# A two-layer decoder trunk with gathered experts: seven gather buffers and nine kept weight chunks in place of eight and seven, with a weight computed per row and a reordered start and end

## What is computed

```
h = rmsnorm(x);  [p | q | k | v | gate logits] = h @ w_in          # 1024 -> 4096
A = pool_mixer(p)            # trailing means over 2/4/8/16 tokens minus the token, per-group map
B = attention(q, k, v) @ w_attn_up                                  # 8 heads, causal, ALiBi
x = x + (sigmoid(gA) * A + sigmoid(gB) * B) @ w_out
t = rmsnorm(x)
for each of 8 PEER heads:
    s = (t @ w_q)[2 halves] @ sub_keys.T           # 2 x 128 key scores
    sv, si = top_k(s, 16) of each half
    cv, ci = top_k(sv[0][:, None] + sv[1][None, :], 16)      # best 16 of 256 sums
    eid = si[0][..] * 128 + si[1][..];  g = softmax(cv)
x = x + sum over 8 heads * 16 experts of  g * gelu(u[eid] . t) * v[eid]
```

## Time and profile before

| | |
|---|---|
| the profiled execution's own time | 1624.07 us |
| its span, first to last instruction | 1622.3 us |
| median of three executions | 1621.58 us (1619.27 to 1624.75) |
| mean granted TensorE clock | 0.955 |
| moved by DMA | 653.94 MB, of which the gathers 536.90 MB |
| TensorE busy | 1323.5 us (82%) |
| VectorE busy | 1098.2 us (68%) |
| ScalarE busy | 756.4 us (47%) |
| GpSimd busy | 597.5 us (37%) |

### The profile page before, as it was taken

How to read it: one execution, slowest core, us unless ns; L and a number is a source line. 1 busy time by engine, 2 the same in 40 slices (tenths; PEclk the granted TensorE clock), 3 DMA queues, 4 the chain that set the end, 5 groups by cost and what they waited for, 6 DMA issues and landing times. The chain is left out here.

```text
span 1622.3 us, 18071 instructions
## 1 busy us (share of the span) xinstructions
PE 1323.5 (82%) x5612; PEld 814.4 (50%) x5612; DVE 1098.2 (68%) x2602; ACT 756.4 (47%) x2833; POOL 597.5 (37%) x516
## 2 busy tenths in 40 slices
PE   7997788888888696977888779888888877778776
PEld 7985456654554264653455436565555433233222
DVE  1057879766588687745567778867656777768545
ACT  1213535445544534424554454544464555555555
POOL 0012333345434332323533343233443444444552
PEclk9999999999999999989999999899999999999999
DMA  7859999999999999999999999999999999999996
GB/s 289 305 232 423 399 422 420 423 422 421 420 422 410 415 389 424 422 424 419 413 421 423 413 409 400 422 424 421 419 413 424 410 414 422 421 418 417 411 422 285
DMA packets 91800, 653.94 MB, mean 403 GB/s; under 512 B 10120, under 2 KB 11576, under 8 KB 12600
## 3 DMA queue, kind: packets, MB, share of 16 engines
q0 software_dynamic: 73728, 536.90, 80.2%
q1 hardware_dynamic: 17976, 115.89, 17.6%
HBM read 651.71 MB, written 1.05 MB: 402 GB/s over the span
## 5 line engine op out<-in xcount | busy, mean ns | idle before, releaser
L597 PE MATMUL ybank<-ring,diag 128*128 128x512 f32 x1668 | 828.2, 639 | 272.9 <-ACT diag L775 267.4
L1123 POOL DMA_INDIRECT ring<-in_uv,expert x512 | 597.3, 1167 | 1003.2 <-DVE xs L1014 435.3
L1001 DVE SCALAR_TENSOR_TENSOR ring<-ring,tok 128x1024 f32<-128x1024 f32 x512 | 620.8, 1225 | 390.7 <-DMA ring<-in_uv,expert 385.2
L597 PEld LDWEIGHTS ybank<-ring,diag 128*128 128x128 f32 x1668 | 314.4, 200 | 695.7 <-ACT diag L775 368.9
L747 ACT ACTIVATE sq<-dots 128x2 f32<-128x2 f32 (+1 forms) x257 | 52.2, 203 | 732.4 <-DVE ring L1001 732.3
L416 PEld LDWEIGHTS bank<-hT,wring 128*128 128x128 f32 x2432 | 291.6, 198 | 27.1 <-issue 27.1
L416 PE MATMUL bank<-hT,wring 128*128 128x128 f32 x2432 | 293.0, 281 | 4.9 <-DVE hT L904 4.9
L763 ACT ACTIVATE wgt<-th,half_p 128x1 f32<-128x1 f32 x512 | 170.3, 379 | 8.6
L775 ACT ACTIVATE diag<-cst,wgt 128x128 f32<-128x128 f32 x417 | 148.2, 392 | 5.2
L757 ACT ACTIVATE th<-arg,dots 128x1 f32<-128x1 f32 x512 | 122.9, 287 | 8.2
L1014 DVE SCALAR_TENSOR_TENSOR xs<-ring,wgt,xs 128x1024 f32<-128x1024 f32 x95 | 121.8, 1282 | 1.9 <-ACT wgt L763 1.8
(11 more groups left out here) (108 smaller groups left out, 681.7 us busy)
## 6 DMA issues: line engine op xcount, KB each, us to landing
wring<-in_chunks SPq DMA_DIRECT2D x92, 1024.0 KB
held<-in_chunks SPq DMA_DIRECT2D x14, 1024.0 KB, 18.6
ring<-in_uv,expert POOLq DMA_INDIRECT x512
xs<-in_x SPq DMA_DIRECT2D x2, 512.0 KB, 12.0
wpool<-in_w_pool SPq DMA_DIRECT2D x2, 512.0 KB, 13.9
trunk_out<-buf SPq DMA_DIRECT2D x4, 256.0 KB, 4.8
cst<-in_consts SPq DMA_DIRECT2D x1, 672.0 KB, 6.4
ring<-in_pool_scale SPq DMA_DIRECT2D x1, 512.0 KB, 8.5
```

Source lines behind the costliest of these rows:

```text
L597: ins = pe.matmul(ybank[m][:, :], diag[:, nth % DIAGS, :], ring[:, (2 * t + r) % RING, D + m * BANK:D + (m + 1) * BANK], start=(nth == ten ...
L1001: dve.scalar_tensor_tensor(out=ring[:, g % RING, 0:D], in0=ring[:, g % RING, 0:D], scalar=1.0, in1=tok[:, :], op0=ALU.mult, op1=ALU.mult, ...
L1123: pool.indirect_dma_start(ring[:, g % RING, :], None, uv, bass.IndirectOffsetOnAxis(ap=expert[:, w % 2, at:at + 1], axis=0)).then_inc(row_ ...
```

## The change

Numbers: `RING` 8 to 7, `HELD` 7 to 9. The kept chunks are then 16 to 24, which takes in the PEER query chunks of heads 0, 1 and 2. Small buffers make the room: `p_sb` shares `qT`, and keeps no first tile, since a new `carry` (128x64) holds what the first tile contributes to the first 16 tokens of the second; `kT` holds one tile, with the second tile's keys in `soft`; `rinv_all` lies in `buf2`; `prob` and `expert` have one window's place instead of two; the constant table loses 448 columns.

Weights of a row: `scalar_tick` runs the whole chain for row 0 when its own dot product is there, and then for row 1. Start: ScalarE issues `cst`, `beside` and `gains`. The query of head 0 runs in one piece behind the last transposes. The first eight experts come from the best 8 of each key half and 64 sums; the full search of head 0 follows, and its second eight experts are picked behind tick 0. End: in the last window TensorE first copies x into `ybank`, and `close_last` adds row 510 to `ybank` and then row 511.

```diff
-HELD = 7
+HELD = 9
-RING = 8
+RING = 7
...
-        first_heads = [(-10, -8, -6), (-2, 0, 1), (2, 3, 5), (7, 9, 10), (12, 13, 15), (17, 18, 20), (21, 23, 24),
+        first_heads = [(-10, -8, 0), (1, 2, 3), (4, 5, 6), (8, 9, 10), (12, 13, 15), (17, 18, 20), (21, 23, 24),
                        (26, 27, 29)]
-        first_queries = (-19, -17, -15, -13, -11, 0, 2, 4)
+        first_queries = (-19, -17, -15, -13, 0, 2, 4, 6)
...
+                        if r == 0 and k in (4, 6):
+                            pe.wait_ge(*read(w, f"g{k // 2 - 1}"))
...
-                side(0, a, range(6))
-                pe.wait_ge(x_mixed, OUTS * w + OUTS)
-                for j in range(2):
-                    ins = pe.transpose(g[:, j * P:(j + 1) * P], x_of(tile)[:, (6 + j) * P:(7 + j) * P], ident)
-                filled("g2", ins)
-                pe.wait_ge(*read(w, "g2"))
-                filled("pq0a", side(0, a, range(6, KC)))
+                filled("pq0a", side(0, claim("pq0a", a_done), range(KC)))
...
+            if tile == 0:
+                b = claim("carry", a_done)
+                for g in range(NG):
+                    lo = C_BEFORE + g * REACH
+                    ins = pe.matmul(b[:, g * REACH:(g + 1) * REACH], p_sb[:, g * P:(g + 1) * P], cst[:, lo:lo + REACH],
+                                    start=True, stop=True)
+                filled("carry", ins)
...
+                if tile == 0:
+                    pe.matmul(b[:, g * P:g * P + REACH], mine, cst[:, first:first + REACH], start=True, stop=True)
+                    ins = pe.matmul(b[:, g * P + REACH:(g + 1) * P], mine, cst[:, lo + REACH:lo + P],
+                                    start=True, stop=True)
...
+            if last and n == 0:
+                pe.wait_ge(x_mixed, OUTS * windows)
+                for m in range(2):
+                    pe.matmul(ybank[m][:, :], ident, x_of(w % NT)[:, m * BANK:(m + 1) * BANK], start=True, stop=False)
...
-            for rows in ((0,), (1,)) if t == windows * TICKS - 1 else ((0, 1),):
-                act.wait_ge(dot_done, 2 * t + rows[-1] + 1)
-                act_stepped(act.activation(sq[:, these], dots[:, c0:c0 + len(rows)], ACT.Square))
...
+            for r, c in enumerate(col):
+                act.wait_ge(dot_done, 2 * t + r + 1)
+                act_stepped(act.activation(sq[:, r:r + 1], dots[:, c:c + 1], ACT.Square))
...
+            def first_experts():
                 for r in range(2):
                     dve.wait_ge(*read(w, f"score0{'ab'[r]}"))
-                    key_search(0, (r,))
-                cand = best_sums(0)
+                    key_search(0, (r,), (0,))
+                sums = tmp[:, 0:64]
+                square = sums.rearrange("p (i j) -> p i j", i=8)
+                all_sums(square, 8)
+                search(lambda r: cv[:, :], lambda r: ci[:, :], lambda r: sums, range(1), (0,))
+                places(8, 3)
+                pick_of(0, 0, 8, square)
...
             if w == 0:
-                first_head()
+                yield head_tick(w, 0, 0)
+                first_experts()
+                key_search(0, eights=(8,))
+                yield head_tick(w, 0, 1)
+                sum_search(0)
+                weigh_heads(0)
+                yield head_tick(w, 0, 2)
+                pick_of(0, 8, 8, tmp[:, 0:P].rearrange("p (k i) -> p k i", i=TOPK))
...
+            t = windows * TICKS - 1
             dve.wait_ge(pe_summed, tensor_rows(t))
+            for r in range(2):
+                g = 2 * t + r
+                dve.wait_ge(wgt_done, vector_rows(t) + r + 1)
...
+                        scalar=wgt[:, g % COLS:g % COLS + 1], in1=part if r else ybank[m][:, :],
...
+                act.dma_start(cst[:, 0:C_DIST], consts[:, 0:C_DIST]).then_inc(ident_in, 16)
+                act.dma_start(beside[:, :], side[0]).then_inc(side_in, 16)
+                act.dma_start(gains[:, :], rows[0]).then_inc(gains_in, 16)
...
-                sp.dma_start(cst[:, 0:C_DIST], consts[:, 0:C_DIST]).then_inc(ident_in, 16)
```

More of the change, by code:

```diff
@@ L473, in tensor_mix @@
                     o, c = (hd % 2) * DH, hd // 2
-                    ins = pe.matmul(b[:, m * S:m * S + sources * P], qT[o:o + DH, c, :],
-                                    kT[o:o + DH, c, 0:sources * P], start=True, stop=True)
+                    for s in range(sources):
+                        its = later_kT[o:o + DH, c // 2, (c % 2) * P:(c % 2 + 1) * P] if s else kT[o:o + DH, c, :]
+                        ins = pe.matmul(b[:, m * S + s * P:m * S + (s + 1) * P], qT[o:o + DH, c, :], its,
+                                        start=True, stop=True)
                 filled(f"qk{n}", ins)
@@ L598, in tensor_tick @@
                                     ring[:, (2 * t + r) % RING, D + m * BANK:D + (m + 1) * BANK],
-                                    start=(nth == tensor_rows(w * TICKS)), stop=(nth == tensor_rows((w + 1) * TICKS) - 1))
+                                    start=(nth == tensor_rows(w * TICKS) and not last), stop=(nth == tensor_rows((w + 1) * TICKS) - 1))
                 ins.then_inc(pe_summed, 1)
@@ L742, in scalar_tick @@
                 act.wait_ge(prob_ready, PH * w + n // (TOPK // 2) + 1)
-            mine, others = rows_on_tensor(t), rows_on_vector(t)
-            for rows in ((0,), (1,)) if t == windows * TICKS - 1 else ((0, 1),):
-                c0, these = col[rows[0]], slice(rows[0], rows[-1] + 1)
-                act.wait_ge(dot_done, 2 * t + rows[-1] + 1)
-                act_stepped(act.activation(sq[:, these], dots[:, c0:c0 + len(rows)], ACT.Square))
[L748 to L751, removed]
+            mine = rows_on_tensor(t)
@@ L758, in scalar_tick @@
+                if r not in mine:
+                    ins.then_inc(wgt_done, 1)
+                    continue
                 act_stepped(ins)
+                nth = tensor_rows(t) + mine.index(r)
                 act.wait_ge(act_step, act_steps[0])
[L760 to L768, removed]
@@ L799, in bank, with search @@
                 return filled_bank(dve, w, name)
-            def search(vals, idxs, data, each):
-                for lo in (0, 8):
+            def search(vals, idxs, data, each, eights=(0, 8)):
+                for lo in eights:
                     if lo:
@@ L812, in search, with key_search, all_sums, places @@
                     settle(dve)
[L814 to L822, removed]
-                settle(dve)
[L824 to L830, removed]
+            def key_search(h, each=range(2), eights=(0, 8)):
+                search(lambda r: sv[:, r, :], lambda r: si[:, r, :], lambda r: score[:, 2 * h + r, :], each, eights)
+            def all_sums(sums, n):
+                step(dve.tensor_tensor(sums, sv[:, 0, 0:n].unsqueeze(2).to_broadcast([P, n, n]),
+                                       sv[:, 1, 0:n].unsqueeze(1).to_broadcast([P, n, n]), ALU.add))
+                step(dve.tensor_copy(sif[:, :, 0:n], si[:, :, 0:n]))
+                settle(dve)
+            def places(n, bits):
+                step(dve.tensor_scalar(cab[:, 0, 0:n], ci[:, 0:n], bits, None, ALU.logical_shift_right))
+                step(dve.tensor_scalar(cab[:, 1, 0:n], ci[:, 0:n], 2 ** bits - 1, None, ALU.bitwise_and))
                 settle(dve)
-                step(dve.tensor_copy(cabf[:, :, these], cab[:, :, these]))
+                step(dve.tensor_copy(cabf[:, :, 0:n], cab[:, :, 0:n]))
                 settle(dve)
```

144 lines of the change are left out of this document (67 added, 77 removed).

## The result

Over 20 executions each, the changed kernel takes 1626.86 us (1620.49 to 1631.99) and the one before 1621.62 us. The ratio is 1.0026, interval [1.0014, 1.0038]: slower by some 4.2 us (5.2 by the medians), where 1610.7 and 0.73 for faster were forecast. It is outside the forecast's own range of 1604 to 1616 and at the very edge of the wide one, 1597 to 1627. The profiled execution has a span of 1624.2 us. A single ratio is known to 0.12 to 0.3%, so a difference of two runs to some 3 us (5 with e4).

A forecast was written before the change was run, and what follows sets the result against it. DMA was taken as the bound: bytes over their rate, plus two ends. Terms -4.7 - 14.9 + 10 - 1.3 = -10.9 us gave 1610.7 us against the median, own range 1604 to 1616, eight in ten 1597 to 1627.

The forecast's parts named there:

- Seven buffers, +10: Row ring: each of four stretches with low DMA share loses one more row's time, 4 x 2.48 = +10 us, bounds 0 to 31.
- the rival that seven are too few: Chunk ticks: when VectorE is behind, three rows out are not enough to feed DMA; 1631.7 us, slower, chance 0.15.
- Kept chunks, -14.9: DMA behind the first gather: four loads fewer and two chunks moved into the prologue, 6.29 MB less, -14.9 us, bounds 0 to 14.9.
- Start and end, -6.0 in sum: Prologue and tail: first gather 4.7 us earlier, at 109.0; -1.3 us at the end by adding row 510 straight onto `ybank`.
- The pooling: TensorE's path in the prologue: 16 more instructions in window 0, +2.0 us, bounds 1 and 2.5.
- The first query and the experts: Before the first gather: query in one piece -1.0 us; first experts from a shorter search -2.4 us.
- the two readings weighed: `beside` issued by ScalarE: small transfer overtakes chunk 0, 3.3 us gained (taken), or only the earlier issue, 0.9 us.
- Per-row chains, 0 on the path by themselves: ScalarE weights per row: rows released about 3.2 and 2.5 us earlier, ScalarE pays 218 us with room; 0 on the path.
- The free ring: Rival on the row ring: seven buffers cost nothing, 1600.7 us, chance 0.26.
- ScalarE: Rival: ScalarE becomes late where mix work meets the longer chains and holds up TensorE; 13 us, 1623.7 us, chance 0.07.
- The rival on the chunks: Kept chunks give no time, ticks being held by VectorE and TensorE; term shrinks to the prologue's 5.0 us, 1620.6, chance 0.06.
- dips of 10 us in sum: Sign in the profile: deeper DMA share dips at the handovers of windows 0 to 2, about 10 us idle, none in window 3.

The follow-up runs named there:

- e4: The kernel before with only `RING = 7`, 7 row buffers in place of 8: 1644.94 us, 1.0168 of the kernel before.
- e2: The changed kernel with the sizes of before, 8 buffers and 7 kept chunks: 1612.86 us, 0.9955 of the kernel before.
- e3: The changed kernel with 7 buffers and 7 kept chunks (only `HELD` differs): 1631.63 us, 1.0065 of the kernel before.
- e5: The changed kernel with VectorE's weighted sum ahead of both dot products of the next tick: 1603.39 us, 0.9893 of the kernel before.
- e8: The changed kernel with 9 buffers and 7 kept chunks: 1613.13 us, 0.9953 of the kernel before.
- e11: The changed kernel with 6 buffers, 10 kept chunks and the weighted sum ahead of both dot products: 1648.85 us, 1.0173 of the kernel before.
- e10: The changed kernel with the weighted sum ahead of both dot products and 7 kept chunks in place of 9: 1616.85 us, 0.9973 of the kernel before.
- e1: The changed kernel with 8 buffers and 8 kept chunks: 1609.32 us, 0.9930 of the kernel before.
- e7: The changed kernel with one ScalarE chain for both rows of a tick, as before: 1631.23 us, 1.0068 of the kernel before.
- e6: The changed kernel with 8 buffers, 8 kept chunks and the weighted sum ahead of both dot products: 1610.00 us, 0.9938 of the kernel before.

## Why the prediction was wrong

By the runs the sum is -7.3 for the start, the end and the per-row chains (e2), +17.8 for the seventh buffer in place of the eighth (e3 against e2) and -6.3 for the kept chunks (the changed kernel against e3), +4.2 us together. The forecast had -6.0, +10 and -14.9. Two terms are off, by 7.8 and by 8.6 us. Each miss alone leaves a gain of 2 to 3 us, which is none by this measurement; both together make it slower.

**Seven buffers, +10: this step failed, 17.8 measured.** The mechanism was named rightly, in this step and in the rival that seven are too few: e5 moves the weighted sum on VectorE ahead of two dot products, frees nothing else and takes the loss away. The error was to price it from the four stretches in which the DMA share of the kernel before was lowest, as if only there a row less would show. By GB/s that kernel already had 24 short stretches of 5 us, and with seven buffers there are 54 (45 in e3). The delays are spread to match: against e2 the dot products of e3 fall behind by 8.8 us over rows 0 to 127, by 2.1 over rows 128 to 255, by 11.5 over rows 256 to 383, and by none after that.

The slack is to be worked out per row; this is an estimate from the durations above. Row 0 of a tick, call it row g, is released behind the dot product of row g + 3. When row g + 3 has landed, four later rows are out with eight buffers and three with seven: 9.9 or 7.4 us of DMA work. Of that go 1.22 and 1.28 us for its dot product and the weighted sum, 0.3 until GpSimd starts and 0.9 for its instruction, 3.7 in all. Seven buffers leave 3.7 us and eight 6.2, less the delay of the transfer's own start and more by 2.48 where a chunk is being loaded. A `sum_search` ahead of those dot products takes 3.6 to 3.8 us (249.40 to 252.98 above, 976.05 to 979.8 in the trace of before). That is all that seven leave, with nothing for the transfer's start, and well within eight. With the attention work behind it, it is 6.5 us in the place shown, a little more than eight leave too, and there e2 has its one short stretch. So it isn't four places that pay but many of the ticks where a piece of mix meets a row of VectorE. e8 and e11 fit the picture on both sides: nine buffers give nothing, six cost much. The estimate was not tried by a run that moves the mix itself.

**Kept chunks, -14.9: failed too, -6.3 at these sizes.** The bytes were right. The term has two parts, 9.9 us for the four reloads not made and 5.0 for the two chunks moved ahead of the first gather. These are the starts of the dot products of some rows (row g has the dot product number g in order of time, from 0), in us, of two pairs of kernels that differ in the kept chunks alone:

| row | e3 (7 kept) | changed (9 kept) | e10 (7 kept) | e5 (9 kept) |
|---|---|---|---|---|
| 0 | 115.54 | 116.19 | 116.39 | 117.67 |
| 48 | 281.94 | 285.78 | 279.79 | 277.45 |
| 96 | 415.83 | 418.14 | 412.93 | 410.67 |
| 112 | 467.16 | 465.02 | 464.07 | 456.73 |
| 352 | 1209.17 | 1204.88 | 1192.88 | 1184.55 |
| 384 | 1304.53 | 1295.31 | 1284.08 | 1271.59 |

The reloads are saved where they would be made, between rows 96 and 112 and between rows 352 and 384: 4.4 and 4.9 us in the changed kernel, 5.1 and 4.2 in e5. That part was right, and it holds while the ring stalls. Over rows 0 to 48 the changed kernel loses 3.2 us on e3, where e5 gains 3.6 on e10. So the step that failed is the chunks moved ahead: 5.0 us forecast, none seen at seven buffers with the old order. These are single executions, and why the first rows lose is not shown. What the runs do show is that the two terms, +10 and -14.9, which were added as if independent, are not: the same two chunks give 6.3 us at one order on VectorE and 13.0 at the other.

With eight buffers one more kept chunk gave 0.25%, 4 us, against 7.5 by bytes (e1 against e2), a difference at the edge of what is known. Here too the reloads show (2.1 us between rows 96 and 112, 3.0 between rows 352 and 384; 5.0 by bytes) and the part moved ahead does not. A reason can only be read from traces: the first gathers go out one per 1.25 us, and the DMA share from 110 to 120 us is 1.02 in e2, where chunks fill that ramp, and 0.86 in e1, where they came earlier.

**Start and end, -6.0 in sum: right**, -7.3 by e2, with the per-row chains in it. `rinv_all` came at 7.76 us, 1 us later than forecast, since `beside` needed about 6.5 us from its issue and the matmul ended 0.5 us later; 2.3 us of the 3.3 came. The pooling cost 1.8 us (2.67 us from its first matmul to the next projection's, before 0.90), 2.0 forecast. The first query and the experts gained more than forecast: from the last piece of x (99.15 us; before 99.62) to the first gather it takes 10.1 us, before 14.1.

`beside` now moves next to chunk 0, which SyncE issues in the same microsecond, and no longer behind it. These are the packets, MB and shares of SyncE's queue (q1) and ScalarE's (q10) from 4.5 to 6.5 us:
```profile
q1 hardware_dynamic: 88, 0.72, 85.5%
q10 hardware_dynamic: 91, 0.10, 13.7%
```
Nearly as many packets of one as of the other agree with the Trainium skill, DMA: Bandwidth & Descriptors, section Queues, rings and completion order, by which each DMA engine goes round between the queue rows packet by packet. Of the two readings weighed, the one by which only the issue time is saved (0.9 us) is not what happened. But `beside` did not overtake chunk 0, as the prediction had it: the last packets of chunk 0 come before 7.0 us, those of `beside` after that, and it is waited for until about 7.7.

**Per-row chains, 0 on the path by themselves:** with seven buffers they save 6.8 us (e7), which bears out that they give TensorE's rows their time back; what they are worth with eight wasn't tried. ScalarE is busy 922.8 us (970 forecast), and e2 shows no loss from it.

**The rivals.** The free ring and ScalarE are out (e3, e2). What happened is the one that had 0.15, at a little over half of its upper price, together with a shortfall on the chunks. The rival on the chunks, with 0.06, had the wrong part of that term: it let the reloads give nothing and kept the 5.0 us of the prologue, and in the traces it is the other way round. I gave each its chance as if only one could occur, and here both terms failed. Of the signs named, dips of 10 us in sum were to come at the handovers; what came is near the other one, dips spread over the windows that have chunk ticks, which was to make the forecast wrong toward the slow side. GpSimd's mean wait for `weighted` is 5.1 us in place of 4.7, as forecast, though e2 has 5.1 as well (483.1 us, 94 times) and no loss.

## What to carry to other kernels

A ring is sized by the longest stay of a row and not by the mean: take the slowest kind of row, add what may stand ahead of its release on that engine, and compare with ring length times the pace; if it doesn't fit, look first whether the releasing instruction can be issued earlier. Moving it here was worth as much as a megabyte of buffer (21.6 us against 17.8, each known to some 3). A wait for a buffer tells little by its length; ask how much DMA work is out when it begins. The gain of fewer bytes and the loss of a shorter queue were not independent here, so they are to be tried together and not added.

## What the runs showed that I had not expected

A digit of 9, or a share of 0.99 to 1.00, can stand over a loss of 3%: the changed kernel's first window has a share of 0.99 at 404 GB/s, where 1.01 goes with 418 to 419. Here the GB/s line is the one to compare, and it would have shown before the prediction that the kernel ran short in more than four places.

The best combination of this study, seven buffers, nine kept chunks and the weighted sum first, is 1.07% faster than the kernel before and 1.33% faster than the changed one. With the weighted sum first, the step from seven to six buffers costs far more than the one from eight to seven, some 45 us (e11 against e5) against 3 (e10 against e2, whose order is the old one; by e6 the order makes no difference at eight).
